# Fifteen unread columns taken off a constants tile

## The reference

```python
h = x @ w_in                                   # per layer: projection
y = concatenate([rms(y_pool), rms(y_chunk), rms(y_sb)]) * g_mix
x = layer_norm(ALPHA * x + y @ w_out, ...)     # layers 0 and 1
f = (silu(x @ wg) * (x @ wu)) @ wd             # dense (0) or per expert (1)
a = maximum(h @ w_up, 0); (a * a) @ w_down     # dense block, layers 2 to 5
```

## Time and profile before

| | us |
|---|---|
| median of 3 runs | 2522.37 |
| lowest, highest | 2519.64, 2527.46 |
| the profiled execution | 2519.64 |
| its span in the profile | 2517.9 |

### The profile page before, as it was taken

One profiled execution on the slowest core, in us unless ns is written; L12 is line 12 of the kernel. 1 busy time (PEld: TensorE's weight loads), 2 busy tenths in 40 slices (PEclk: granted clock), 3 DMA queues, 4 the chain that ended last, 5 costly groups with the idle time before them and its releaser, 6 DMA issues. The chain is left out here.

```text
span 2517.9 us, 33705 instructions
## 1 busy us (share of the span) xinstructions
PE 2462.2 (98%) x13444; PEld 2095.7 (83%) x13444; DVE 1716.1 (68%) x1892; ACT 1438.4 (57%) x1603; POOL 80.2 (3%) x94
## 2 busy tenths in 40 slices
PE   8999999999999999999999999999999999999998
PEld 6889978788888888888877789878998789887897
DVE  5565465788898898888975754566556665557654
ACT  6344353588888888888855444454444544445442
POOL 0000010000000000000000200000000000002000
PEclk9999999999999999999999999999999999999999
DMA  9156552599999999999955165452655155552552
GB/s 308 65 193 207 186 188 70 199 352 353 349 339 349 338 348 354 330 350 348 353 186 189 68 219 191 172 172 92 209 193 180 68 199 189 184 176 80 197 184 101
DMA packets 241907, 555.49 MB, mean 221 GB/s; under 512 B 10760, under 2 KB 36768, under 8 KB 241440
## 3 DMA queue, kind: packets, MB, share of 16 engines
q1 hardware_dynamic: 241696, 552.40, 63.3%
HBM read 551.30 MB, written 1.07 MB: 219 GB/s over the span
## 5 line engine op out<-in xcount | busy, mean ns | idle before, releaser
L1822 DVE TENSOR_TENSOR wlo<-raw,whi 128x2048 fp32r<-128x2048 f32 x488 | 1118.5, 2300 | 460.8 <-ACT whi L1452 460.1
L1452 ACT ACTIVATE whi<-raw 128x2048 fp32r<-128x2048 f32 x488 | 935.7, 1924 | 569.6 <-issue 149.0
L931 PE MATMUL bank<-xt_hi,wlo 128*128 128x256 f32 x1056 | 298.8, 283 | 0.0
L931 PE MATMUL bank<-xt_lo,whi 128*128 128x256 f32 x1056 | 298.8, 283 | 0.0
L931 PE MATMUL bank<-xt_hi,whi 128*128 128x256 f32 x1056 | 298.8, 283 | 0.0
L777 PE MATMUL bank<-whi,xt_hi 128*128 128x512 f32 (+1 forms) x528 | 204.2, 387 | 6.4 <-DVE wlo L1828 3.0
L931 PEld LDWEIGHTS bank<-xt_lo,whi 128*128 128x128 f32 x1056 | 202.6, 192 | 1.1
L931 PEld LDWEIGHTS bank<-xt_hi,whi 128*128 128x128 f32 x1056 | 202.6, 192 | 1.1
L931 PEld LDWEIGHTS bank<-xt_hi,wlo 128*128 128x128 f32 x1056 | 202.6, 192 | 0.0
L777 PE MATMUL bank<-wlo,xt_hi 128*128 128x512 f32 (+1 forms) x528 | 198.2, 375 | 0.0
L777 PE MATMUL bank<-whi,xt_lo 128*128 128x512 f32 (+1 forms) x528 | 198.2, 375 | 0.0
(11 more groups left out here) (304 smaller groups left out, 4096.1 us busy)
## 6 DMA issues: line engine op xcount, KB each, us to landing
raw<-in_moe_wg SPq DMA_DIRECT2D x88, 1024.0 KB, 6.1
raw<-in_moe_wu SPq DMA_DIRECT2D x88, 1024.0 KB, 6.0
raw<-in_moe_wd SPq DMA_DIRECT2D x88, 1024.0 KB, 5.8
raw<-in_mlp_w_up SPq DMA_DIRECT2D x64, 1024.0 KB, 5.3
raw<-in_mlp_w_down SPq DMA_DIRECT2D x64, 1024.0 KB, 4.9
raw<-in_diff_w_in SPq DMA_DIRECT2D x24, 1024.0 KB, 5.4
raw<-in_w_in SPq DMA_DIRECT2D x19, 1024.0 KB, 8.0
raw<-in_moba_w_in SPq DMA_DIRECT2D x12, 1024.0 KB, 5.1
```

Source lines behind the costliest of these rows:

```text
L931: mm = pe.matmul(bank[b + f // 2][:, f % 2 * S:(f % 2 + 1) * S], w[:, k, f * P:(f + 1) * P], a[:, kx, :], start=(kx == 0 and i == 0 and f ...
L1452: act.activation(whi[u % NH][:, :], raw[u % NR][:, :], ACT.Copy).then_inc(hi_ready[u % NR], 2)
L1822: dve.tensor_tensor(wlo[u % NR][:, :], raw[u % NR][:, :], whi[u % NH][:, :].bitcast(F32), ALU.subtract).then_inc(lo_ready[u % NR], 2)
```

## The change

```diff
@@ line 156
 C_INV = C_IOTA + 8
 C_HALF = C_INV + 8
 C_ONECOL = C_HALF + 16
-C_N = C_ONECOL + 16
+C_N = C_ONECOL + 1
```

## The result

The changed kernel takes 2540.32 us, median of 4 runs (2538.09 to 2541.99), against 2522.07 us (2519.64 to 2527.46, 4 runs) before: a ratio of 1.0069, interval 1.0057 to 1.0082. That is slower by 18 us, outside the predicted range, whose upper end was 2532. The profiled execution took 2538.81 us, 19.2 more than that of before.

The account below looks back on a forecast made before the run. TensorE, 98% busy, was taken to bound the kernel. The profiled 2519.6 us + 0 + 0 + 0 stayed 2519.6, which as a median gave a forecast of 2522 us, range 2514 to 2532.

Parts of the forecast that it names:

- What bounds the kernel: Whole kernel: TensorE, busy 2462.2 of 2517.9 us (98%), sets the time; only slower instructions or later feeding can change it.
- First, the constants' transfer and the identity: Start of the kernel: narrower constant rows in HBM; taken as 0, upper ends 2.8 us (constants) and 1.6 us (identity).
- The bound of 2.8 us from `toep`: Constants' transfer: slowed as `toep` packets are against weight packets (82 against 46 ns), 0.8 x 3.5 = 2.8 us at most.
- the threshold that the prediction set for the constants' rows: In 30 to 60 us, TensorE idle time above 0.5 us would show the constants' rows to be at fault.
- Second, the tiles: Tiles behind `cst` start 32 bytes lower in SBUF: taken as 0, upper end the first rival's 39 us.
- The rival with the line of 64 bytes: Engines read SBUF in 64-byte lines; moved stationary operands cost 6.7 ns per matmul; 2561 us if nothing hides it; chance 0.10.
- Its count of 4008 matmuls: Executed matmuls with a moved stationary operand in lines 845, 1165 and 1087, together 26.9 us.
- its other terms: Same rival: attention, transposes and allowance 912 x 6.7 ns = 6.1 us; VectorE and ScalarE operations 5.8 us.
- Its variant in which the loads of stationary operands lie beneath the matmul before them: Same rival with loads hidden: the 26.9 us vanish, 12 us remain, 2534 us.
- Third, the places in HBM: Other arrays may move because `in_cst` is 7680 bytes smaller; matters only in the expert layer, either sign; taken as 0.
- that rival: Expert layer: weights from a worse HBM place, rate 2% lower, 750 us into 765, total 2537 us; chance 0.05.

Follow-up runs that it names:

- pad_cst: The changed kernel with an unused 32-byte tile behind `cst`, so every tile lies where it lay before the change: 2522.1 us against 2521.5, ratio 1.0000.
- the sweeps: Three versions of the kernel before, with `xt_*`, `h_*`, `e_*`, `odd_*` at various byte distances from the weight streams: 2533.80, 2533.42 and 2531.57 us against 2521.29.
- all streams apart: The kernel before with 32 bytes ahead of `raw0` and behind `whi3`, so `raw`, `wlo`, `whi` start 32 bytes off all other tiles: 2540.01 us, ratio 1.0071.

## Why the prediction was wrong

**What bounds the kernel: right.** TensorE sets the time, and all of the loss is in its instructions.

**First, the constants' transfer and the identity: right.** The DMA issues of the first 60 us (KB, us to landing) after the change:

```profile
...
cst<-in_cst SPq DMA_DIRECT2D x1, 1168.5 KB, 13.4
...
cst<-in_cst SPq DMA_DIRECT2D x1, 64.0 KB, 1.9
```

They were 13.3 and 2.0, and TensorE's first wait is 5.3 us for 5.4. The bound of 2.8 us from `toep` was not needed; whatever makes `toep` slow, its row pitch in HBM is not shown to be it. TensorE's idle time in 30 to 60 us is 1.3 us instead of 0.5, above the threshold that the prediction set for the constants' rows. By this reading alone one would have blamed them; the kernel with `pad_cst`, which keeps the narrow constants and loses nothing, has 29.56 us busy in this window and shows otherwise.

**Second, the tiles: this step failed.** The prediction set it to 0 "by the rows nearest to it", lines 503, 507, 508 and the short matmuls. For VectorE and ScalarE that was right: line 503 has 286 ns for 285 now, and

```profile
...
L1575 ACT ACTIVATE z<-z,nmx 128x256 f32<-128x256 f32 x76 | 37.7, 496 | 0.0
...
L2470 DVE TENSOR_TENSOR h_lo<-h_f,h_hi 128x1024 fp32r<-128x1024 f32 x28 | 34.2, 1220 | 4.5 <-ACT h_hi L1648 4.5
```

stand at 496 and 1220. For TensorE those rows were no evidence. They were read by the absolute start of one operand, and what counts is the distance between two; and they are of 8 and 16 moving columns, while the effect is +6 ns at 512 columns and -3 at 256. The trace of before held no wide matmul with two operands at different places modulo 256 bytes, so the term had no nearest row at all, and its bound should have kept its weight. It was worth 22.0 us at the paces; the expert layer hid about 3.5 of them, and the span grew by 19.1.

**The rival with the line of 64 bytes** named the place (the moved stationary operands) and nearly the price (6.7 ns, measured 6.0), and its sign to watch for, "a pace of 234 ns for h_* and odd_* alone", came true. Its mechanism is refuted: shifting everything costs nothing, and a step of a whole 64 or 128 bytes costs about as much as one of 32 (233.3 and 232.4 ns against 233.2). Its count of 4008 matmuls also took in the 192 of line 1087 with 256 columns at the price of the 512. With it its other terms fall: attention and transposes (6.1 us) kept their paces, 109 ns even for `z` in line 1357, which moved while the `cst` beside it didn't; VectorE and ScalarE (5.8 us) didn't move, and the 256-column form changed its sign. Its variant in which the loads of stationary operands lie beneath the matmul before them and hide everything is wrong too: the loads are listed with 188 ns beside a pace of 227.3, and the pace grew by 6.0 ns all the same. So its 2561 was too high and its 2534 too low.

The Trainium skill has lines of 16 bytes in SBUF — State Buffer, section Specifications (TRN2). The prediction read from it that a shift by 32 bytes costs nothing. For the absolute start the runs agree (ratio 1.0005); for the distance between operands the rule is silent, and there they show up to 6 ns. In TensorE: Matmul & The Clock Gate, section Step-by-step: what each phase is for, the Trainium skill says that TensorE reads the moving operand and the stationary one through two independent ports, so that a load takes nothing from the running matmul. In these runs the pace depends on where the two start relative to each other, by 2.6%, which that rule doesn't lead one to expect; no run shows what couples them.

**Third, the places in HBM: right at 0.** The DMA share of 500 to 1250 us fell from 0.98 to 0.97 and the rate from 347 to 343 GB/s, which by itself would look like that rival. But the kernel with `pad_cst` has the same places in HBM and no loss, and ScalarE waits less for weights, not more; the lower rate goes with the slower TensorE.

**What stays open.** Why the period is 256 bytes, why the map has 230.7 ns at 8 and 229 at 192 between slower neighbours, and why the 256-column form gains by what the 512-column form loses: a meeting of the two reads would be a natural guess, but no run shows what happens inside. Why line 937 got 117.6 ns where line 1087 had 115.3. Of the 1.0 us that the two first attention stages grew, the run with `pad_cst`, where no tile behind it moved, has 0.4 and the run with only `h_*` moved 0.5 too, so part of it is scatter from run to run; the rest has no experiment of its own. No run varied the type of the operands, and the sweeps are of one execution each.

## What to carry to other kernels

Before an edit changes the size of any tile in SBUF, list which pairs of stationary and moving operands it moves relative to each other, modulo 256 bytes; in this kernel, bound by TensorE with fp32r operands, 32 bytes cost 0.7%, and a chosen distance gave 0.4% back below where it started. Read absolute place and distance as two different questions, and take a row as evidence for a wide matmul only if it is one. Where no row shows a term, leave its bound in the range rather than take the value of rows that are merely alike.

## What the runs showed of the hardware

- A matmul of 512 moving fp32r columns behind its own load takes 227.3 ns from start to start when both operands start at the same place modulo 256 bytes, and 229 to 233.4 ns otherwise, already at a distance of 4 bytes (232.2).
- With 256 moving columns the same place gives the slowest pace, 119.9 ns, and a distance of 64 or 224 bytes 115.3 to 117.6. In the transposes of line 1357, with 128 columns of plain fp32, the distances 0 and 224 can't be told apart, 109 ns both times.
- A common shift of all operands by 32 bytes changes nothing (2522.22 against 2521.5 us), nor does a row of constants that starts at an odd multiple of 4 bytes in HBM (13.4 against 13.3 us to landing).
- In the expert layer, where the transfers are busy at 0.98, idle time of TensorE took up about 3.5 of 11.2 us of slower matmuls, and 5 to 6 of 17.0 in the kernel with all streams apart.
